# Two layers of a hybrid decoder trunk on one core: two unequal opening copies, and layer 0's weight tiles requested fewer projections ahead

## The reference

```python
h = rms_norm(x, norm_g)
proj = jnp.einsum('btd,de->bte', h, w_in)
a_val, a_glu, a_gate, b_val, b_gate, q, k, v, c_gate = jnp.split(proj, cuts, axis=-1)
# A: u = a_val * sigmoid(a_glu), causal depthwise convolution of width 31, LayerNorm, silu, times silu(a_gate)
# B: trailing means over 2, 4, 8, 16 positions, a small linear map, times silu(b_gate)
# C: attention over keys at distances 0..128, 4*(0..128), 16*(0..128), times silu(c_gate)
new_k = jnp.concatenate([k_buf, k], axis=1)[:, -2048:]      # and new_v the same
```

## Time and profile before

| | |
|---|---|
| Median of 3 runs | 399.57 us (398.87 to 400.03) |
| Time of the profiled execution | 398.96 us |
| Its span | 397.1 us |
| PE / PEld / DVE / ACT / POOL busy | 86% / 68% / 58% / 25% / 15% of the span |
| DMA | 157.73 MB in 44329 packets, mean 397 GB/s |
| Mean granted TensorE clock | 0.946 |

### The profile page before, as it was taken

How to read it: one execution, slowest core, us unless ns; L and a number is a source line. 1 busy time by engine, 2 the same in 40 slices (tenths; PEclk the granted TensorE clock), 3 DMA queues, 4 the chain that set the end, 5 groups by cost and what they waited for, 6 DMA issues and landing times.

```text
span 397.1 us, 4745 instructions
## 1 busy us (share of the span) xinstructions
PE 343.2 (86%) x1550; PEld 270.0 (68%) x1550; DVE 232.3 (58%) x530; ACT 100.1 (25%) x237; POOL 58.5 (15%) x110
## 2 busy tenths in 40 slices
PE   3897799998879859989958999999979867989990
PEld 2676578886557646578847888888747644658880
DVE  2603769759975996431013489978985997540110
ACT  4300013542523122411011011453352222230011
POOL 4007740003400011044001320000600002000000
PEclk9999989999969898999996999999978998989997
DMA  8999999999999999999999999999999999999982
GB/s 300 422 414 402 419 417 403 419 421 414 420 419 417 420 415 401 409 413 416 411 404 415 417 418 409 421 421 417 421 419 417 416 386 355 376 396 384 389 346 87
DMA packets 44329, 157.73 MB, mean 397 GB/s; under 512 B 6988, under 2 KB 20116, under 8 KB 44306
## 3 DMA queue, kind: packets, MB, share of 16 engines
q0 software_dynamic: 14624, 88.25, 54.5%
q10 hardware_dynamic: 14420, 41.52, 26.4%
q1 hardware_dynamic: 15262, 27.67, 18.7%
HBM read 140.23 MB, written 104.46 MB: 616 GB/s over the span
## 4 chain that ended last, share of the span: by engine, by line
PE 50%; DVE 14%; SPq 12%; DMA 10%; issue 5%; ACTq 4%; ACT 4%; DVEq 0%
PE pj L704 24%; PE pj L847 14%; SPq L491 11%; DMA kg<-in_cache_k_win 10%; DVE yc L1307 3%; PE psc L776 3%; PE ptr L622 3%; DVE ssc L1251 2%; ACTq L471 1%; PE ps L824 1%; ACTq L885 1%; DVE spsum_pad L1277 1%; DVE tok L1245 1%; DVE sc L1213 1%; PE ps L830 1%
## 5 line engine op out<-in xcount | busy, mean ns | idle before, releaser
L704 PE MATMUL pj<-hT,wt 128*128 128x264 f32 x800 | 195.5, 403 | 7.4 <-DVE hT L1162 5.0
L704 PEld LDWEIGHTS pj<-hT,wt 128*128 128x128 f32 x800 | 157.0, 200 | 39.7 <-issue 12.7
L1307 DVE SCALAR_TENSOR_TENSOR yc<-u_ext,par,yc 128x256 f32<-128x256 f32 x180 | 77.2, 480 | 3.8 <-DVE u_smp L1191 1.0
L847 PE MATMUL pj<-mix,wt 128*128 128x264 f32 x256 | 61.1, 395 | 0.0
L847 PEld LDWEIGHTS pj<-mix,wt 128*128 128x128 f32 x256 | 49.2, 195 | 8.4
L611 POOL DMA_DIRECT2D out<-in_cache_v_win x48 | 26.2, 553 | 143.3 <-issue 143.3
L1377 DVE TENSOR_TENSOR xT<-xT,pj 128x264 f32<-128x264 f32 x16 | 6.9, 430 | 55.2 <-PE pj L847 55.2
L611 POOL DMA_DIRECT2D out<-in_cache_k_win x48 | 26.4, 557 | 82.0 <-issue 82.0
L965 ACT ACTIVATE ex<-pj 128x264 f32<-128x264 f32 x22 | 8.6, 390 | 77.1 <-PE pj L704 44.0
L1245 DVE TENSOR_TENSOR tok<-kg,qb 128x1536 f32<-128x1536 f32 x10 | 17.6, 1758 | 4.2 <-DMA kg<-in_cache_k_win 3.7
L1189 DVE SCALAR_TENSOR_TENSOR u_ext<-ex,pj 128x256 f32<-128x256 f32 x6 | 2.5, 421 | 29.9 <-ACT ex L965 29.9
(11 more groups left out here) (187 smaller groups left out, 334.8 us busy)
## 6 DMA issues: line engine op xcount, KB each, us to landing
wt<-in_w_tiles ACTq DMA_DIRECT2D x62, 512.0 KB, 32.3
out<-in_cache_k_win POOLq DMA_DIRECT2D x24, 1080.0 KB, 44.4
out<-in_cache_v_win POOLq DMA_DIRECT2D x24, 1080.0 KB, 81.3
out<-in_cache_k_win POOLq DMA_DIRECT2D x8, 1200.0 KB, 72.0
out<-in_cache_v_win POOLq DMA_DIRECT2D x8, 1200.0 KB, 89.3
out<-in_cache_k_win POOLq DMA_DIRECT2D x16, 432.0 KB, 64.2
out<-in_cache_v_win POOLq DMA_DIRECT2D x16, 432.0 KB, 87.3
kg<-in_cache_k_win SPq DMA_DIRECT2D x32, 144.0 KB, 33.5
```

The lines of the kernel that those rows point to most:

```text
L704: last = nc.tensor.matmul(pj[n % RING][:, 0:T], wt[:, g % WRING, k, :], hT[:, k, :], start=(k == 0), stop=(k == KD - 1))
L847: last = nc.tensor.matmul(pj[n % RING][:, 0:T], wt[:, g % WRING, k, :], mix[:, k, :], start=(k == 0), stop=(k == KD - 1))
L1307: last = V.scalar_tensor_tensor(out=yc[:, t, 0:SEQ], in0=x_w, scalar=par[:, ROW_CW + w * CT + t:ROW_CW + w * CT + t + 1], in1=yc[:, t, 0:S ...
```

## The change

The constants of the tiles are new: SyncE requests three tiles (0 to 2), ScalarE tiles 3 and 4 at the start and 5 to 8 behind the state loads. In layer 0, tile n + 9 is requested behind projection n up to n = 8 (tiles 9 to 17), two tiles behind each of projections 9 to 13 (2n and 2n + 1, so 18 to 27), and n + 14 from n = 14 on as before. The first two main copies of K, layer 1, first sample, had 768 rows each (48 blocks on 16 engines); they now have 384 rows (24 blocks) and 1152 rows (72 blocks), and their outermost dimension is 8 and not 16, so that each runs on 8 DMA engines. Bytes and sizes of the pieces stay as they were.

```diff
-SP_TILES, ACT_TILES = 4, (6, 10)
+SP_TILES, ACT_TILES = 3, (5, 9)
+LEAD = 9
+HALVES_CUT = 8 * 3 * DEEP_STEP
+def engines_of(l, kind, s, a):
+    return 8 if (l, kind, s) == (DEPTH - 1, "k", 0) and a < FAR_LO else 16
+def main_zones(l, kind, s):
+    if engines_of(l, kind, s, 0) == 8:
+        return (0, HALVES_CUT), (HALVES_CUT, FAR_LO)
+    return ((0, FAR_LO // 2), (FAR_LO // 2, FAR_LO)) if (kind, l) in DEEP else ((0, EVEN_CUT), (EVEN_CUT, EVEN_ROWS))
 def copies_of(l):
     return [(kind, s, a, b) for kind in ("k", "v") for s in range(NS)
-            for a, b in (*(((0, FAR_LO // 2), (FAR_LO // 2, FAR_LO)) if (kind, l) in DEEP else ((0, EVEN_CUT), (EVEN_CUT, EVEN_ROWS))),
-                         (FAR_LO, GATHER[0][0]))]
+            for a, b in (*main_zones(l, kind, s), (FAR_LO, GATHER[0][0]))]
+def tiles_behind(n):
+    if n < LEAD:
+        return (n + LEAD,)
+    if n < WRING:
+        return 2 * n, 2 * n + 1
+    return (n + WRING,)
...
-                        dst, src = (t.rearrange("(c e f) h d -> c e (f h d)", c=16, f=DEEP_STEP)[:, :, 0:(DEEP_STEP - 1) * C_ATT]
+                        dst, src = (t.rearrange("(c e f) h d -> c e (f h d)", c=engines_of(l, kind, s, a), f=DEEP_STEP)[:, :, 0:(DEEP_STEP - 1) * C_ATT]
...
-                        if l == 0 and n == 0:
-                            for g in range(ACT_TILES[1], WRING):
-                                next_tile(g)
-                        next_tile(l * NRING + n + WRING)
+                        for g in tiles_behind(l * NRING + n):
+                            next_tile(g)
```

More of the change, by code:

```diff
@@ L233 @@
           1: {("proj", NPROJ - 2): (0,), ("proj", NPROJ - 1): (1,), **{("wout", m): (m + 2,) for m in range(KD - 2)}}}
+def tiles_behind(n):
[4 more added lines that the diff above has]
+    return (n + WRING,)
+assert ACT_TILES[1] == LEAD
+assert [g for n in range(WRING) for g in tiles_behind(n)] == list(range(LEAD, 2 * WRING))
+assert all(max(tiles_behind(n)) - WRING <= n for n in range(WRING))
 def deep_count(kind, l):
```

## The result

In one series on the same chip the changed kernel took 401.5 us (median of 7 runs, 400.48 to 402.89), the kernel before 399.07 (398.06 to 400.03): ratio 1.0061, 95% interval [1.0041, 1.0081]. Forecast was 398.2 with a range up to 402.4, so the time lies in the range and on the other side of no change. The profiled execution of after took 400.48 us, its span is 398.7.

A forecast was written before the change was run, and what follows sets the result against it. The backlog of one slow DMA engine was taken to end the kernel. Lighter opening copies gain 1.4 us and the tiles nothing, so 399.57 - 1.4 = 398.2 us; range 396.9 to 402.4.

The forecast's parts named there:

- part 1: Opening K-cache copies of layer 1: unequal copies on two halves of the DMA engines relieve the slowest; 1.4 us gained.
- 24 blocks on 8 engines are 3 an engine, and 72 on 8 are 9: Opening copies: one half of the engines carries 3 blocks less than before, the other 3 more, a 2.7 us shift.
- The first would end at 396.1 - 2.7: Kernel's end: the slowest DMA engine, given the light copy, ends at 393.4; the second slowest then ends last at 394.9.
- (b): Rival on the opening copies: the heavy copy falls on the slowest engine, which ends 2.7 us later; 402.3 us, chance 0.14.
- (d): Rival at the end: the slowest engine's lag is no sum of its packets, or re-forms; 399.6 us, chance 0.14.
- (e): Rival: the compute path becomes the end, ScalarE held over projections 10 to 13; 400.7 us, chance 0.06.
- part 2: Layer 0 weight tiles: requesting fewer ahead removes early holds; costed at nothing on the time, ends 0.5 gain or loss.
- 1.7 us of issue: Behind projections 9 to 13: ten tile requests of 0.33 us in place of five cost ScalarE 1.7 us more.
- a hold until 80 to 84: Tile 27's request, behind projection 13, is held until tile 17 or 18 has landed, at 80 to 84 us.
- up to 2: Compute path in layer 0: it loses up to 2 us if the holds do not fall into slack.
- 84 to 86: Start of `tok` on VectorE, in us, as expected in the changed profile; before it was 87.89.
- 2 gained: Compute path in layer 0: 2 us taken as gained, from 3.8 gained to up to 2 lost.

The follow-up runs named there:

- changed_reversed: Changed kernel with its two opening copies in the other order, 72 blocks first and then 24; 403.71 us, ratio 1.0043 to the kernel before.
- parts_light: Changed kernel's tiles, the 96 opening blocks as six interleaved DMAs of 8 shares, 24 blocks then 72; 401.38 us, ratio 0.9976 to the kernel before.
- parts_even: Changed kernel's tiles, the 96 opening blocks as six interleaved DMAs of 16 shares, 48 and 48; 400.33 us, ratio 0.9947 to the kernel before; repeated 0.9963.
- copies_only: Kernel before with only the two new opening copies, 24 then 72 blocks, tiles as before; 403.17 us, ratio 1.0019 to the kernel before.
- copies_reversed: Kernel before with the new opening copies as 72 then 24 blocks, tiles as before; 403.33 us, ratio 1.0024 to the kernel before.
- halves_light: Kernel before with the 96 blocks in 18 unmergeable DMAs on eight engines each, alternating, one-piece (24-block) DMAs first; 404.16 us, ratio 1.0085 to the kernel before.
- halves_heavy: Kernel before with the 96 blocks in 18 unmergeable DMAs on eight engines each, alternating, three-piece (72-block) DMAs first; 404.77 us, ratio 1.0099 to the kernel before.
- changed_even: Changed kernel with opening copies of 48 and 48 blocks; 400.61 us, ratio 0.9972 to the kernel before; repeated on another chip 0.9976.
- changed_again: Changed kernel unaltered, measured once more on another chip; 403.74 us, ratio 1.0041 to the kernel before.
- changed_32_64: Changed kernel with opening copies of 32 and 64 blocks, 16 engines each; 400.71 us, ratio 0.9974 to the kernel before.
- profiles of part 2: Second group of follow-up runs, on one chip: both kernels unaltered, and the changed one with 48 and 48 or 72 and 24 blocks; before 402.21 us.
- before_again: Kernel before, unaltered, run again under its own name; 402.55 us, ratio 0.9996 to the kernel before.
- tiles_only: Changed kernel with the opening copies as before, 48 and 48 blocks on 16 engines; 400.86 us, ratio 0.9965 to the kernel before.
- lead_ten: Changed tiles with 48 and 48 blocks, but tile 3 back on SyncE's queue and requests ten ahead; 402.28 us, ratio 0.9989 to the kernel before.
- copies_even: Kernel before with 48 and 48 blocks through the changed copy code, tiles as before; 402.35 us, ratio 1.0012 to the kernel before.
- parts_heavy: Changed kernel's tiles, the 96 opening blocks as six interleaved DMAs of 8 shares, 72 blocks then 24; 402.7 us, ratio 1.0014 to the kernel before.

## Why the prediction was wrong

**The failed step** is the first of part 1: "24 blocks on 8 engines are 3 an engine, and 72 on 8 are 9". They were 2 and 6, on twelve engines each. So no half was relieved: eight engines had 8 blocks in place of 6, and the four engines that each copy left out had 96 packets without data together. No rival of the prediction had that the change doesn't do what it says. Its sum would have been 2 x 0.90 = 1.8 us later. With the tiles' ratio and the 399.07 of before in the same series, 0.9972 x 399.07 = 398.0, this gives 399.8, and 400.6 with the 0.8 us of longer packets; 401.5 was measured, so 0.9 has no name. What is settled: the twelve engines are what was built; copies on all sixteen (32 and 64 blocks, 48 and 48) cost nothing; and on the changed tiles copies on twelve or eight cost 0.3 to 0.8% in each of the five forms tried. Whether by their unequal bytes or by the packets without data stays open. That the cost is the sum of these two terms is arithmetic, not shown: changed_reversed has the first and not the second.

**A second step failed where the halves were true**: "The first would end at 396.1 - 2.7". I took the lateness of the slowest engine for a sum that carries over from opening to end. parts_light has 5 blocks in place of 6 on the lower half if the first DMA starts at engine 0; it ought to have been 0.9 us faster than parts_even and was 1.05 slower. Why is not shown: the other half may end last instead, or the packets without data may have delayed the copies. Nor need a lead last: of four shares about 5 us ahead at copy 10 of copies_only (-5.2 to -4.8) two are left at copy 22 (-5.9 and -5.4, the next at -2.1), though in after all four are (-5.1 to -3.2).

**Rivals.** (b) came near in size (402.3), but its condition, a second copy on eight engines of its own, wasn't built. copies_reversed and changed_reversed don't refute it, as the same eight engines are the heavy ones in either order; halves_light and halves_heavy, only 0.6 us apart, speak against it. (d), the lag re-forms, fits copies_only, as just told. (e), the compute path as the end, has its sign: the last output store is issued 2.6 us later, after 391. But changed_even and changed_again, on one chip and with the same tiles, issue it at 393.59 and 393.62, with 3.1 us between their medians; and changed_32_64 issues it at 394.78 and its span is 398.9, against 391.82 and 398.7 in after. So (e) isn't what the copies cost.

**Tiles, part 2.** Right: ScalarE's and TensorE's early holds go, and the keys stop being late. Mis-sized: the double requests. I had 1.7 us of issue and a hold until 80 to 84 that costs "up to 2"; three of them took 3.31 + 5.14 + 5.02 = 13.5 us. Hence `tok` at 90.13 and not at 84 to 86: the "2 gained" were 2.2 lost against the earlier trace rows. The profiles of part 2, all of one chip, read otherwise: `tok` starts at 90.14 in before_again, 88.77 in changed_even and 90.51 in changed_again, so in those profiles the tiles alone gain 1.4 and the copies take it back. Costed at nothing, with 0.5 as the most it could gain, the part brings 0.24 to 0.35% in four comparisons (tiles_only, changed_even twice, changed_32_64), 1.0 to 1.4 us, and 0.37 and 0.53% with six DMAs. No run shows by what way it reaches the end. lead_ten points to tile 3's place and the keys, but with overlapping intervals.

**Also open.** On the tiles of before the same copies cost 1.0019 and 1.0024, and copies_even, where nothing is moved, reads 1.0012; on the changed tiles they cost 1.0069. The parts don't add there (0.9965 x 1.0019 = 0.9984 against 1.0041 and 1.0061), and no run says why; with the halves they do (1.0085 x 0.9965 = 1.0050 against 1.0051).

## What to carry to other kernels

Count the engines of a DMA from the access pattern as it is built: dimensions that touch are merged, and a written outermost 8 ended here as 24, on twelve engines. Compare the packet counts of the two pages as well: packets that came on top without bytes gave away the twelve engines. Where all DMA engines are busy to the end, let each copy run on all sixteen; on the changed tiles copies on fewer, meant to help a late engine, lost in every form tried here. Before a test of one property (uneven shares), look for what else the form brings (packets without data), and build the control for it. And spread requests: two tiles behind one projection held ScalarE for 3 to 5 us from projection 11 on, with all that stands behind on it, though the earlier requests as a whole still gained.

## What the runs showed of the hardware that was not expected

- A GpSimd copy reports sixteen shares even when twelve engines carry data: four of copy 0 in changed_reversed were 7.5 us ahead of the median, and stayed about 7 ahead in copy 2. The engines left out get 4-byte packets instead of data: 96 in all with 24 and 72 blocks on twelve engines, 288 in parts_light on eight. Each takes 9 to 11 ns and one of queue 0's turns.
- In four profiles with copies on eight or twelve engines (after, changed_again, parts_light, parts_heavy) the sixteen engines were as busy and moved less: 383 to 400 GB/s against 408 to 423 with even copies on the same tiles in 10 to 30; and 354 in 30 to 40 of halves_light. In changed_reversed, copies_only and copies_reversed they didn't, or hardly did.
- With 24 and 72 blocks GpSimd takes 5.00 to 5.02 us to issue its eight first copies in all five kernels, where the earlier trace rows have 4.74 (the line is of after):

```profile
1.88 5.00 POOL L640 DMA_DIRECT2D out<-in_cache_k_win  x8 [1.43 <-issue]
```
